# mLSTM scores and numerators as three fp32r products of two-part operands, with every low part taken on VectorE

## What is computed

```python
qk = silu(causal_depthwise_conv(concat([q_m, k_m]), conv_w, conv_b))
w_intra = exp(dmat - m_t) * einsum('bhtd,bhsd->bhts', q, k)
num = w_inter * einsum('bhtd,bhde->bhte', q, C) + einsum('bhts,bhse->bhte', w_intra, v)
den = w_inter * einsum('bhtd,bhd->bht', q, n) + sum(w_intra, axis=-1)
h = num / maximum(abs(den), exp(-m_t))
```

## Time and profile before

| what | value |
|---|---|
| median of 3 runs | 1985.76 us (1985.33 to 1986.19) |
| the profiled execution's own time | 1984.43 us |
| its span | 1982.6 us |
| TensorE busy | 1943.9 us (98%) |
| VectorE busy | 1058.0 us (53%) |
| ScalarE busy | 637.9 us (32%) |
| GpSimd busy | 273.5 us (14%) |
| granted TensorE clock, mean | 0.994 |

### The profile page before, as it was taken

One profiled execution on the slowest core, in us unless ns is written; L12 is line 12 of the kernel. 1 busy time (PEld: TensorE's weight loads), 2 busy tenths in 40 slices (PEclk: granted clock), 3 DMA queues, 4 the chain that ended last, 5 costly groups with the idle time before them and its releaser, 6 DMA issues.

```text
span 1982.6 us, 23955 instructions
## 1 busy us (share of the span) xinstructions
PE 1943.9 (98%) x9770; PEld 1591.8 (80%) x9770; DVE 1058.0 (53%) x1481; ACT 637.9 (32%) x1063; POOL 273.5 (14%) x178
## 2 busy tenths in 40 slices
PE   8999999999999999999999999999999999999997
PEld 6788878888888888888888778877777878888886
DVE  6777543345455644344344666767776554344346
ACT  5332222233333432222234422234444342222222
POOL 2221210011111111010014011110101131011012
PEclk9999999999999999999999999999999989999999
DMA  4222233332221323333323222321211313233222
GB/s 168 97 75 85 85 92 100 98 83 77 83 64 49 122 90 99 99 96 96 96 88 108 64 75 75 106 67 63 64 49 49 118 58 100 96 96 100 93 79 80
DMA packets 54549, 172.68 MB, mean 87 GB/s; under 512 B 6027, under 2 KB 11603, under 8 KB 54440
## 3 DMA queue, kind: packets, MB, share of 16 engines
q1 hardware_dynamic: 53056, 169.93, 27.1%
q10 hardware_dynamic: 1384, 1.22, 0.2%
HBM read 168.91 MB, written 2.22 MB: 86 GB/s over the span
## 4 chain that ended last, share of the span: by engine, by line
PE 87%; DVE 8%; ACT 3%; issue 1%; DMA 0%; POOL 0%; SPq 0%; DVEq 0%
PE PS L1185 26%; PE PS L1187 25%; PE PS L1186 25%; DVE WL L1901 1%; PE PS L1323 1%; PE PS L1338 1%; PE PS L1525 1%; PE PS L1361 1%; PE PS L1503 1%; PE PS L1291 1%; DVE AR L2050 1%; PE PS L1370 1%; PE PS L1384 1%; PE PS L1547 1%; ACT WH L1594 1%
## 5 line engine op out<-in xcount | busy, mean ns | idle before, releaser
L1185 PE MATMUL PS<-HH,WH 128*128 128x512 f32 x1368 | 539.9, 395 | 8.3 <-DVE WL L1901 8.3
L1187 PE MATMUL PS<-HH,WL 128*128 128x512 f32 x1368 | 534.2, 391 | 0.0
L1186 PE MATMUL PS<-HL,WH 128*128 128x512 f32 x1368 | 533.8, 390 | 0.0
L1594 ACT ACTIVATE WH<-RAW 128x1024 fp32r<-128x1024 f32 (+2 forms) x322 | 326.7, 1015 | 424.5 <-PE PS L1187 423.9
L1901 DVE TENSOR_TENSOR WL<-RAW,WH 128x1024 fp32r<-128x1024 f32 (+2 forms) x262 | 325.7, 1243 | 226.7 <-ACT WH L1594 224.3
L1185 PE MATMUL PS<-AH,WH 128*128 128x512 f32 x1080 | 426.0, 394 | 0.5 <-DVE AL L1892 0.5
L1187 PE MATMUL PS<-AH,WL 128*128 128x512 f32 x1080 | 421.4, 390 | 0.0
L1186 PE MATMUL PS<-AL,WH 128*128 128x512 f32 x1080 | 421.2, 390 | 0.0
L1185 PEld LDWEIGHTS PS<-HH,WH 128*128 128x128 f32 x1368 | 257.9, 188 | 62.9 <-DVE WL L1901 8.3
L1187 PEld LDWEIGHTS PS<-HH,WL 128*128 128x128 f32 x1368 | 257.6, 188 | 54.4
L1186 PEld LDWEIGHTS PS<-HL,WH 128*128 128x128 f32 x1368 | 258.0, 189 | 52.1
(11 more groups left out here) (256 smaller groups left out, 1496.1 us busy)
## 6 DMA issues: line engine op xcount, KB each, us to landing
RAW<-wst SPq DMA_DIRECT2D x290, 512.0 KB, 3.5
RAW<-wst SPq DMA_DIRECT2D x24, 256.0 KB, 2.5
RAW<-wst SPq DMA_DIRECT2D x8, 384.0 KB, 2.9
XT<-xT SPq DMA_DIRECT2D x3, 512.0 KB, 7.2
AR<-mx SPq DMA_DIRECT2D x4, 256.0 KB, 5.8
AR<-scr SPq DMA_DIRECT2D x16, 64.0 KB, 4.4
AR<-scr SPq DMA_DIRECT2D x8, 128.0 KB, 4.9
AR<-w SPq DMA_DIRECT2D x2, 512.0 KB, 4.0
```

Of the source, the lines that this page charges most:

```text
L1185: T.matmul(out, wh, XH[:, k, :], start=k == 0, stop=False)
L1186: T.matmul(out, wh, XL[:, k, :], start=False, stop=False)
L1187: m = T.matmul(out, wl, XH[:, k, :], start=False, stop=k == nk - 1)
L1594: t = A.activation(WH[:, i % NW, 0:n], RAW[:, i % NR, 0:n], ACT.Copy, scale=1.0)
```

## The change

Queries, keys, values and weights of the mLSTM are kept as two fp32r parts each: the high part is the value rounded by ScalarE, the low part what is left of it, subtracted on VectorE. Each f32 product becomes three fp32r products (high by high, high by low, low by high), as for the projections. A query or key unit has three steps behind it instead of two (tanh; product; high and low part), with two buffers for the tanh; a value unit's transposed tokens are copied by ScalarE and subtracted by VectorE. Numerators have 258 columns, the last two both from the ones. The weights' parts lie in rows 6 and 7 of AH and AL and in two small tiles. Queries, keys and values have one pair of buffers instead of two buffers of f32. In head 0 `weights` comes right behind the scores, with no quarter between; its high parts come one quarter later and its low parts four. The diff, cut to its core:

```diff
-PARTS = {"qm": 2, "km": 2, "vm": 1, "om": 1, "va": 1, "ga": 1, "gb": 1, "pb": 1, "small2": 1, "gk": 2, "gv": 1,
+PARTS = {"qm": 3, "km": 3, "vm": 2, "om": 1, "va": 1, "ga": 1, "gb": 1, "pb": 1, "small2": 1, "gk": 2, "gv": 1,
          "gr": 1, "ks": 2, "kw": 2, "vs": 1, "vw": 1, "mg": 1, "mn": 1, "pn": 1}
-        fill.quarters(4)
+        fill.quarters(4 if h else 0)
         e.weights(h)
-        fill.quarters(12 if h else 8)
+        fill.quarters(1)
+        e.weights_hi(h)
+        fill.quarters(3)
+        e.weights_lo(h)
+        fill.quarters(8)
 ...
+        QH, QL, KH, KL = (rounded(4608 + 1024 * n, 1024) for n in range(4))
+        VH, VL = (heads_of(rounded(8704 + 1032 * n, 1032)) for n in range(2))
+        th1 = part(2328, 512)
+        wh2, wl2 = (rounded(2840 + 256 * n, 256) for n in range(2))
+        TH = [th_, th1]
+        WTH = [AH[:, 6, :], AH[:, 7, 0:384], wh2, AH[:, 7, 384:512]]
+        WTL = [AL[:, 6, :], AL[:, 7, 0:384], wl2, AL[:, 7, 384:512]]
+        def th_of(i):
+
+            return TH[CONVS.index(i) % 2]
 ...
             def scores(s, h, blocks):
-                q, k = hq[h % 2], hk[h % 2]
-                for c in (0, 1):
-                    pe.wait_ge(*at("mq", unit_of("qm", 2 * h + c)))
-                    pe.wait_ge(*at("mq", unit_of("km", 2 * h + c)))
                 for t_ in blocks:
                     x, a = SCORES[t_]
                     b, n = s.bank["scores", h, x], 512 - 128 * t_
                     s.free("scores", h, x)
                     for c in (0, 1):
-                        t = T.matmul(PS[:, b, a:a + n], k[:, c * 512 + t_ * 128:c * 512 + t_ * 128 + 128],
-                                     q[:, c * 512 + t_ * 128:c * 512 + 512], start=c == 0, stop=c == 1)
+                        keys, queries = (slice(c * 512 + t_ * 128, c * 512 + e_) for e_ in (t_ * 128 + 128, 512))
+                        pe.wait_ge(*at("m_lo", unit_of("qm", 2 * h + c)))
+                        pe.wait_ge(*at("m_hi", unit_of("km", 2 * h + c)))
+                        T.matmul(PS[:, b, a:a + n], KH[:, keys], QH[:, queries], start=c == 0, stop=False)
+                        T.matmul(PS[:, b, a:a + n], KH[:, keys], QL[:, queries], start=False, stop=False)
+                        pe.wait_ge(*at("m_lo", unit_of("km", 2 * h + c)))
+                        t = T.matmul(PS[:, b, a:a + n], KL[:, keys], QH[:, queries], start=False, stop=c == 1)
                     t.then_inc(*pe_done["mlstm"].next("scored", h, t_))

             def numerators(s, h):
-                v = heads_of(hv[h % 2])
                 pe.wait_ge(*at("ones"))
                 pe.wait_ge(*at("free", "tokens", unit_of("vm", 2 * h)))
                 pe.wait_ge(*at("free", "tokens", unit_of("vm", 2 * h + 1)))
@@ -1333,9 +1350,11 @@
                     b = s.bank["numer", h, t_]
                     s.free("numer", h, t_)
                     for x in range(t_ + 1):
-                        o = wo[x] + (t_ - x) * 128
-                        pe.wait_ge(*at("weights", h, x))
-                        t = T.matmul(PS[:, b, 0:257], WT[:, o:o + 128], v[:, x, :], start=x == 0, stop=x == t_)
+                        o = slice((t_ - x) * 128, (t_ - x) * 128 + 128)
+                        pe.wait_ge(*at("weights_lo", h, x))
+                        T.matmul(PS[:, b, 0:258], WTH[x][:, o], VH[:, x, :], start=x == 0, stop=False)
+                        T.matmul(PS[:, b, 0:258], WTH[x][:, o], VL[:, x, :], start=False, stop=False)
+                        t = T.matmul(PS[:, b, 0:258], WTL[x][:, o], VH[:, x, :], start=False, stop=x == t_)
                     t.then_inc(*pe_done["mlstm"].next("summed", h, t_))
 ...
                 if name in ("qm", "km") and p == 1:
                     act.wait_ge(*at("conv", i, 3))
-                    A.activation(th_, yc, ACT.Tanh, scale=0.5).then_inc(*act_done["mlstm"].next("tanh", i))
+                    if CONVS.index(i) > 1:
+                        act.wait_ge(*at("m_lo", CONVS[CONVS.index(i) - 2]))
+                    A.activation(th_of(i), yc, ACT.Tanh, scale=0.5).then_inc(*act_done["mlstm"].next("tanh", i))
+                elif name in ("qm", "km") and p == 3:
+                    h, c = j // 2, slice(j % 2 * 512, j % 2 * 512 + 512)
+                    act.wait_ge(*at("m_full", i))
+                    if h:
+                        act.wait_ge(*at("scored", h - 1, 3))
+                    t = A.activation((QH if name == "qm" else KH)[:, c], th_of(i), ACT.Copy, scale=1.0)
+                    t.then_inc(*act_done["mlstm"].next("m_hi", i))
+                elif name == "vm" and p == 1:
+                    if j > 1:
+                        act.wait_ge(*at("summed", j // 2 - 1, 3))
+                    act.wait_ge(*at("turned", i))
+                    t = A.activation(VH[:, :, j % 2 * 128:j % 2 * 128 + 128], heads_of(PS[:, s.bank["tokens", i], :]),
+                                     ACT.Copy, scale=1.0)
+                    t.then_inc(*act_done["mlstm"].next("v_hi", i))
 ...
                 if h:
-                    act.wait_ge(*at("summed", h - 1, 3))
+                    act.wait_ge(*at("weights_lo", h - 1, 3))
+            def weights_hi(s, h):
+                if h:
+                    act.wait_ge(*at("summed", h - 1, 3))
+                for t_ in range(4):
+                    n, o = 512 - 128 * t_, wo[t_]
+                    act.wait_ge(*at("weights", h, t_))
+                    t = A.activation(WTH[t_], WT[:, o:o + n], ACT.Copy, scale=1.0)
+                    t.then_inc(*act_done["mlstm"].next("weights_hi", h, t_))
 ...
                 if name in ("qm", "km"):
                     if p == 2:
-                        h, c = j // 2, j % 2
-                        dst = (hq if name == "qm" else hk)[h % 2][:, c * 512:(c + 1) * 512]
+                        x = th_of(i)
                         dve.wait_ge(*at("tanh", i))
-                        if h > 1:
-                            dve.wait_ge(*at("scored", h - 2, 3))
-                        t = V.scalar_tensor_tensor(out=dst, in0=th_, scalar=1.0, in1=yc, op0=ALU.add, op1=ALU.mult)
-                        t.then_inc(*dve_done["mlstm"].next("mq", i))
+                        t = V.scalar_tensor_tensor(out=x, in0=x, scalar=1.0, in1=yc, op0=ALU.add, op1=ALU.mult)
+                        t.then_inc(*dve_done["mlstm"].next("m_full", i))
+                    elif p == 3:
+                        c = slice(j % 2 * 512, j % 2 * 512 + 512)
+                        dve.wait_ge(*at("m_hi", i))
+                        XH, XL = (QH, QL) if name == "qm" else (KH, KL)
+                        t = V.tensor_tensor(XL[:, c], th_of(i), f(XH[:, c]), ALU.subtract)
+                        t.then_inc(*dve_done["mlstm"].next("m_lo", i))
+                elif name == "vm":
+                    if p == 2:
+                        c = slice(j % 2 * 128, j % 2 * 128 + 128)
+                        dve.wait_ge(*at("v_hi", i))
+                        t = V.tensor_tensor(VL[:, :, c], heads_of(PS[:, s.bank["tokens", i], :]), f(VH[:, :, c]),
+                                            ALU.subtract)
+                        t.then_inc(*dve_done["mlstm"].next("free", "tokens", i))
 ...
+            def weights_lo(s, h):
+                for t_ in range(4):
+                    n, o = 512 - 128 * t_, wo[t_]
+                    dve.wait_ge(*at("weights_hi", h, t_))
+                    t = V.tensor_tensor(WTL[t_], WT[:, o:o + n], f(WTH[t_]), ALU.subtract)
+                    t.then_inc(*dve_done["mlstm"].next("weights_lo", h, t_))

             def numerators(s, h):
```

20 lines of the change are left out of this document (10 added, 10 removed).

## The result

The changed kernel takes 1989.99 us (median of 9 runs, 1988.67 to 1991.55), the kernel before 1985.33 (9 runs, 1984.04 to 1986.19). The ratio is 1.0026, with a 95% interval from 1.0017 to 1.0034: slower by 0.26%, or 4.7 us, where the forecast was no change and a range up to 1988.2.

What follows compares the result with a forecast made beforehand. TensorE was taken as the bound, 87% of the chain that ended last. -5.0 + 3.0 + 0.5 + 0.3 + 0.3 = -0.9 us gave 1984.9 us, no change; range over all cases 1981.0 to 1988.2.

Steps and rivals of the forecast that it cites:

- TensorE's own work, -5.0: mLSTM, four heads: fp32r scores save 0.54 us and numerators 0.72 us a head, together 5.0 us less.
- third rival: Weight loads not hidden for short products: each record pays 0.11 us more, giving 1992.8 us; chance 0.02.
- The pause before the columns, +3.0: Before head 0's scores: last key's low part waits for GpSimd's subtraction, so gate columns start 3.0 us later.
- The clock, +0.3: Head 0's scores after the pause: longer pause may lengthen or bury the low-clock stretch; +0.3 us, between -1.6 and +1.6.
- Upstream, +0.5: Ahead of the last convolution: two more low parts in VectorE's queue, one pushing gate scans into GpSimd's subtraction; +0.5 us.
- In heads 2 and 3 VectorE has room; cost 0: Loops with heads 2 and 3: VectorE's added 4.4 us per head fits in its room; cost 0.
- second rival: VectorE becomes the bound between head 0 and head 1; with two GpSimd collisions 1989.5 us; chance 0.09.
- Head 0's weights: Moved ahead of the next unit's eviction, into time VectorE waited; not awaited before, so nothing gained on TensorE.
- The +0.3 at the border to head 1: Head 1's scores wait for the last key's low part at their sixth record; 0.3 us, between 0 and 2.2.
- first rival: The pause before head 0's gate columns stays as it is, the eviction not held; 1980.8 us; chance 0.15.

Runs made afterwards that it cites:

- third: Changed kernel with all lower parts of the mLSTM units' weights made on VectorE, none on GpSimd; 1982.52 us, ratio 0.999 to the kernel before.
- seventh experiment: Kernel before, without the change, with all lower parts of the mLSTM units' weights on VectorE; 1987.68 us against 1985.59, ratio 1.0012.
- experiments 1, 4 and 9: Changed kernel with one edit each: ones and zeros early (1.0012); head 0's weights at their old place (1.0041); units 23 and 31's lower parts on VectorE (1.0014).
- first experiment: Changed kernel with the ones and zeros written earlier, before the third unit's last products; 1987.11 us against 1984.29 for the kernel before, ratio 1.0012.
- tenth experiment: Changed kernel with ones and zeros early, head 0's last key's parts behind unit 7's eviction, units 23 and 31's lower parts on VectorE; 1981.62 us, ratio 0.9984.

## Why the prediction was wrong

It said no change, 1984.9 us; measured are 1989.99. Step by step:

- **TensorE's own work, -5.0.** Right in kind, a little too large: 1.14 us a head and not 1.26, so -4.6. Numerators gave 0.77 (said 0.72). Scores gave 0.37 (said 0.54; 0.27 in head 1): the first step from f32 transposes to an fp32r product is 0.32 us and not 0.227 (117.33 to 117.65), and the 384-column ones show the like (0.26). Between the third and seventh experiment it is 4.4 by the ratios, 4.1 by the traces. The 128-column records start 0.11 apart, as taken; loads are hidden, and the third rival is out.
- **The pause before the columns, +3.0.** The mechanism held instruction by instruction, with the low part at 2.48 us (said 2.3) and L1721 as releaser. Its size was 3.8: GpSimd's subtraction ended at 70.43, 3.4 us behind the third vector product's start, where the earlier trace rows have 2.6. The weight split on ScalarE that starts GpSimd began at 66.90, 0.15 us ahead of that product, and 0.91 ahead of it before: the upstream low parts had pushed the convolution, its tanh and the split back. I had kept the old distance, and priced the push as a step of its own.
- **The clock, +0.3.** Measured 0.8 (0.31 on the columns, about half a microsecond on the scores), within the bounds. In the three other traces with the same instructions here (experiments 1, 4 and 9) it is 1.4, 0.5 and 0.6, so a single trace does not fix this term. In the changed kernel the granted clock was 0.96 from 70 to 72 us, with TensorE at a standstill since 67.9, and then at its lower level, 1.2 GHz, as the window shows:

```profile
72.00:78.00 6.00, 5.34 (x20) 4.75 (x21) 3.53 (x8) 3.70 (x9) 0.00 (x0) 0.50 0.87 288
```

- **Upstream, +0.5.** The chain was 0.74 late, but because of the ones: it vanished in the first experiment. What the low parts push there shows in the pause; 3.0 + 0.5 was forecast for both together, and 3.8 measured.
- **The ones and zeros.** No step at all. The diff shows two memsets turned into two `tensor_scalar`; I priced what was large and passed over them as small. They cost 2.3 us (1.58 + 0.74): a second term that the sum put at nothing, without a reason.
- **"In heads 2 and 3 VectorE has room; cost 0".** This is the step that failed most: 2.7 us, in the pauses at 164 and 218, in the loops of heads 1 and 2, ahead of the scores of heads 2 and 3. Room was there, 1.7 us idle just before. But the cost was not VectorE's work; a low part of 0.68 us moved the next instruction into GpSimd's subtraction, twice in a row in each loop: first the key's product (at 154.05 and 208.12), which took the room, then L2122, which made the pause. The second rival's argument "as many as before, and most of the waits are in the old times already" counted GpSimd's instructions, 22 in both kernels, where what matters is which VectorE instruction meets them and who waits behind it. That rival gave 1989.5, nearly the result, by two such collisions, but put them at the border from head 0 to head 1, where the loss is about 0.1 us; that its number fits is luck.
- **Head 0's weights.** "This gives nothing on TensorE" holds against the kernel before, not within the change: without it the numerators wait 2.4 us. The +0.3 at the border to head 1 came to about 0.1 in the changed kernel and to 0.6 in the tenth experiment.

In sum -4.6 + 3.8 + 0.8 + 2.3 + 2.7 - 0.6 for small steps + 0.1 at the border = 4.5 us over, against 4.7 measured.

The first rival (1980.8, 5.0 us under, chance 0.15) was what the change could give if nothing were held; the tenth experiment comes to 3.2 to 3.8 us under, with 0.7 us more than before still left in front of the columns and 0.6 at the border.

What stays open: what sets the time at which the clock falls and rises again around head 0's scores, where executions with the same instructions differ by 0.9 us. How much the low parts of queries and keys would cost on another engine was not tried.

## What to carry to other kernels

List, on the engine that shares with GpSimd, every instruction between GpSimd's start and the next eviction that TensorE awaits, small ones first of all: an instruction's price there is the rest of GpSimd's, not its own size. Adding work to a half-idle engine shifts all that stands behind it, so look at what the shifted ones will run beside, and not at the busy share. If three or four collisions are found, moving each of them (3.2 to 3.8 us under the kernel before) does at least as well as taking the helper engine away from one stage (1.8 to 3.2 under), and far better than taking it away everywhere (7 over).
